# A hybrid attention and Mamba block on one core: first stage cut into halves and steps, small projection feature-major, decay mask moved to a multiplication

## What is computed

```
mod = silu(c) @ ada_w + ada_b            # six rows of 1024: shift, scale, gate, twice
h = rms_norm(x, g0) * (1 + sc_m) + sh_m
proj = h @ w_in                          # q, kv_lat (256), q_idx, k_idx (64), w_idx (8), z, xbc, dt_raw (32), gates
c_kv = rms_norm(kv_lat, kv_norm_g);  k_idx = rms_norm(k_idx, kidx_norm_g)
att = sparse attention over the 256 best keys of each query
# Mamba-2 in chunks of 128 tokens, per head:
a_cum = cumsum(dt * a)
decay = exp(where(l >= s, a_cum[l] - a_cum[s], -inf))
y_diag = (C B^T * decay) @ (x * dt)
x = x + gt_m * rms_norm(merged(att, ssd) @ w_out, g1);  x = x + gt_f * rms_norm(mlp(...), g3)
```

## Time and profile before

| what | before |
|---|---|
| median of 3 runs | 2412.16 us |
| the profiled execution, own time | 2412.21 us |
| its span | 2410.4 us |
| PE busy | 2327.9 us (97%) |
| DVE busy | 1328.8 us (55%) |
| ACT busy | 723.3 us (30%) |
| POOL busy | 953.3 us (40%) |
| chain that ended last, by engine | PE 90%, DVE 5%, issue 2%, ACT 2%, DMA 1% |
| granted TensorE clock, mean | 0.996 |

### The profile page before, as it was taken

The page is one execution under the profiler, slowest core; times in us unless marked ns, Lnnn a source line. Parts: engine busy times, 40 slices in busy tenths (PEclk is TensorE's granted clock), DMA queues, the critical chain, the costliest instruction groups (busy, mean ns, idle before and its releaser), DMA issues.

```text
span 2410.4 us, 31914 instructions
## 1 busy us (share of the span) xinstructions
PE 2327.9 (97%) x12022; PEld 1919.5 (80%) x12022; DVE 1328.8 (55%) x1956; ACT 723.3 (30%) x1362; POOL 953.3 (40%) x630
## 2 busy tenths in 40 slices
PE   3999999998999999999999999999999999999997
PEld 2977888885557988888887888899888888888886
DVE  4259999995657167585767555334532322322325
ACT  5144121105652234435365111035511212112112
POOL 2221233237672463654554344446332333233222
PEclk9999999999999999999999999999999999999999
DMA  7111452225652113131222553334211111111103
GB/s 274 36 35 45 148 183 87 93 91 168 202 172 68 40 62 127 45 138 46 88 101 102 182 175 119 109 106 162 84 35 53 52 52 35 52 52 40 47 35 79
DMA packets 144732, 230.30 MB, mean 96 GB/s; under 512 B 7956, under 2 KB 111732, under 8 KB 143604
## 3 DMA queue, kind: packets, MB, share of 16 engines
q1 hardware_dynamic: 119936, 166.11, 20.8%
q10 hardware_dynamic: 23684, 59.06, 6.4%
q0 software_dynamic: 1008, 3.67, 0.9%
HBM read 176.39 MB, written 52.43 MB: 95 GB/s over the span
## 4 chain that ended last, share of the span: by engine, by line
PE 90%; DVE 5%; issue 2%; ACT 2%; DMA 1%; ACTq 0%; DVEq 0%
PE ps L652 88%; DVE score L1737 2%; DVE probT L1820 1%; DVE mod_sum L1664 1%; PE ps L877 1%; PE ps L914 1%; PE ps L981 1%; ACT decay L1510 0%; PE ps L700 0%; DMA gate_d<-last_spill 0%; DMA rows_b<-in_ssm_norm_g_dram 0%; ACT L1510 0%; DVE prob L1803 0%; DVE acc L1959 0%; DVE a_lo L1873 0%
## 5 line engine op out<-in xcount | busy, mean ns | idle before, releaser
L652 PE MATMUL ps<-a_hi,w_hi 128*128 128x512 f32 x1728 | 676.7, 392 | 1.7 <-DVE a_lo L1873 1.2
L652 PE MATMUL ps<-a_lo,w_hi 128*128 128x512 f32 x1728 | 672.8, 389 | 0.0
L580 POOL CAST w_hi<-raw 128x2048 fp32r<-128x2048 f32 x90 | 174.7, 1941 | 1179.2 <-issue 859.2
L652 PE MATMUL ps<-a_hi,w_lo 128*128 128x512 f32 x1728 | 543.1, 389 | 0.0
L584 POOL TENSOR_TENSOR w_lo<-raw,w_hi 128x512 fp32r<-128x512 f32 (+1 forms) x360 | 521.5, 1481 | 7.2
L2029 DVE TENSOR_TENSOR x_tm<-x_tm,ps 128x1024 f32<-128x1024 f32 x120 | 146.5, 1221 | 453.8 <-PE ps L652 453.1
L652 PEld LDWEIGHTS ps<-a_hi,w_hi 128*128 128x128 f32 x1728 | 324.5, 188 | 69.6 <-DVE a_lo L1873 1.9
L652 PEld LDWEIGHTS ps<-a_hi,w_lo 128*128 128x128 f32 x1728 | 324.4, 188 | 67.9
L652 PEld LDWEIGHTS ps<-a_lo,w_hi 128*128 128x128 f32 x1728 | 324.5, 188 | 66.2 <-issue 0.2
L652 PE MATMUL ps<-w_hi,a_hi 128*128 128x256 f32 (+1 forms) x896 | 259.1, 289 | 4.4 <-DVE a_lo L1873 2.7
L652 PE MATMUL ps<-w_lo,a_hi 128*128 128x256 f32 (+1 forms) x896 | 253.6, 283 | 0.0
(11 more groups left out here) (255 smaller groups left out, 3033.1 us busy)
## 6 DMA issues: line engine op xcount, KB each, us to landing
raw<-in_w_in_dram SPq DMA_DIRECT2D x35, 1024.0 KB, 5.0
ada_raw<-in_ada_w_dram SPq DMA_DIRECT2D x16, 1024.0 KB, 8.7
raw<-in_w_up_dram SPq DMA_DIRECT2D x16, 1024.0 KB, 5.4
raw<-in_w_down_dram SPq DMA_DIRECT2D x16, 1024.0 KB, 4.7
gates<-gate_d SPq DMA_DIRECT2D x12, 1024.0 KB, 4.9
act_raw<-acts_d ACTq DMA_DIRECT2D x20, 512.0 KB, 5.4
ada<-in_ada_w_dram SPq DMA_DIRECT2D x8, 1024.0 KB, 20.5
acts_d<-decay ACTq DMA_DIRECT2D x16, 512.0 KB, 4.3
```

The source lines that it names most:

```text
L580: nc.gpsimd.tensor_copy(hi, src).then_inc(hi_made, 1)
L652: return nc.tensor.matmul(o, a, b, start=start, stop=stop)
```

## The change

1. SP loads tokens 0 to 511 first, then `ada_w` (its last piece in two halves), the kv block, and only then tokens 512 to 1023.
2. ACT squares, roots and scales the first four tiles; it squares the other four after that, and DVE scales these. `mod_sum`'s last product comes in two halves of 1024 columns, and PE sums each half as it comes. DVE reads the sums in PSUM itself; part of `gain` is made ahead.
3. PE turns six tiles before the sums (banks `FIRST_TURN`), then runs 60 more transposes whose result nobody reads (`IDLE_TURNS`), then the sums.
4. The kv projection goes by feature tiles (`kv_step`): tile `k` of the first four token tiles is multiplied as soon as its split is there, between the turns of the rest.
5. The small projection has its weights (104 columns) as the stationary operand and 512 tokens moving; ACT copies the result to `small_fm`, and PE turns it back (`small_turns`) inside the next block.
6. In `segments` the two `past_bf` matmuls are gone. ACT takes relu(a_cum[s] - a_cum[l]) from PSUM for 8 heads, then one exponential of minus that over 1024 columns. DVE multiplies bank 7 with the triangle `tri` into `cb_sb` in `mix_in`, which takes the place of ACT's copy.

```
-            for t in range(NT):
-                sp.dma_start(x_tm[:, t, :], x[0, t * P:(t + 1) * P, :]).then_inc(x_landed[t], 16)
+            load_tokens(range(4))
             for k in range(KT):
-                sp.dma_start(ada0[:, k, :], ...)
+                if k < KT - 1:
+                    sp.dma_start(ada0[:, k, :], ...)
+            for half in range(2):
+                c = slice(half * D, half * D + D)
+                sp.dma_start(ada0[:, KT - 1, c], ada_w[0, D - P:D, c]).then_inc(ada_last if half else ada_in[KT - 1], 16)
             load(0, cols(w, C_KV))
+            load_tokens(range(4, NT))
...
-            norm_turn(0, range(4))
-            pe.wait_ge(mod0_summed, 1)
+            norm_turn(0, range(6), banks=FIRST_TURN)
+            for i in range(IDLE_TURNS):
+                nc.tensor.transpose(ps[:, 1, (i % 4) * P:(i % 4 + 1) * P], x_tm[:, i % 4, 0:P], ident[:, :])
             for m in range(2 * KT):
-                last = mm(ps[:, 3, m:m + 1], mod_sum[:, m * P:(m + 1) * P], ones[:, 0:1], start=True, stop=True)
+                if m % KT == 0:
+                    pe.wait_ge(mod0_summed, m // KT + 1)
+                last = mm(ps[:, 0, m:m + 1], mod_sum[:, m * P:(m + 1) * P], ones[:, 0:1], start=True, stop=True)
...
+            def kv_step(k, tokens):
+                pe.wait_ge(h_split, tokens[0] // 4 * KT + k + 1)
+                for t in tokens:
+                    last = tm_token(0, t, ps[:, t // 2, (t % 2) * R:(t % 2) * R + R], R, ks=(k,), half=t % 2)
+                return last
+            for k in range(KT):
+                norm_turn(0, (6 + k,), banks=FIRST_TURN)
+                pe.wait_ge(w_split[0], k * LO_PARTS // KT + 1)
+                kv_step(k, range(4))
+            norm_turn(0, (14, 15), banks=FIRST_TURN)
+            for k in range(KT):
+                last = kv_step(k, range(4, NT))
...
-            for t in range(NT):
-                last = tm_token(1, t, ps[:, 4 + t // 4, (t % 4) * NSM:(t % 4) * NSM + NSM], NSM)
+            for k in range(KT):
+                wh, wl = (w_tile(w, 1, k, 0, NSM, NSM) for w in (w_hi, w_lo))
+                for q in range(2):
+                    r = slice(q * 512, q * 512 + 512)
+                    mm(ps[0:NSM, 6 + q, :], wh, a_hi[:, k, r], start=(k == 0))
+                    mm(ps[0:NSM, 6 + q, :], wh, a_lo[:, k, r])
+                for q in range(2):
+                    last = mm(ps[0:NSM, 6 + q, :], wl, a_hi[:, k, q * 512:q * 512 + 512], stop=(k == KT - 1))
...
                     if k >= 1:
-                        pe.wait_ge(decay_done, g * NT + k)
+                        pe.wait_ge(decay_done, 2 * (g * NT + k) - 1)
...
-                        mm(o.rearrange("p (h l) -> p h l", h=4), ident_bf[:, :],
-                           past_bf[:, :].rearrange("p (o l) -> p o l", o=1).broadcast_to([P, 4, P]), start=True)
...
-                        if k >= 1:
-                            act.wait_ge(mix_ready, g * NT + k)
-                        nc.scalar.copy(cb_sb[:, :], ps[:, 7, 0:P]).then_inc(cb_out, 1)
                         if k >= 2:
                             act.wait_ge(mix_done, g * NT + (k - 1))
                         for h in range(HG):
-                            ins = nc.scalar.activation(decay[k % 2][:, h, :], ps[...], ACT.Exp, bias=acum[...])
+                            ins = nc.scalar.activation(decay[k % 2][:, h, :], ps[...], ACT.Relu, bias=dta[...], scale=-1.0)
                         ins.then_inc(decay_done, 1)
+                        act.wait_ge(decay_done, 2 * (g * NT + k) + 1)
+                        nc.scalar.activation(decay[k % 2][:, :, :], decay[k % 2][:, :, :], ACT.Exp, scale=-1.0).then_inc(decay_done, 1)
...
-                    dve.wait_ge(decay_done, g * NT + (k + 1))
+                    dve.wait_ge(seg_done, g * NT + (k + 1))
+                    if g or k:
+                        dve.wait_ge(mix_ready, g * NT + k)
+                    ve.tensor_tensor(cb_sb[:, :], ps[:, 7, 0:P], tri[:, :], ALU.mult).then_inc(cb_out, 1)
+                    dve.wait_ge(cb_out, g * NT + (k + 1))
+                    dve.wait_ge(decay_done, 2 * (g * NT + k + 1))
                     ve.tensor_tensor(decay[k % 2][:, :, :], decay[k % 2][:, :, :],
                                      cb_sb[:, :]...broadcast_to([P, HG, P]), ALU.mult).then_inc(mix_ready, 1)
```

More of the change, by code:

```diff
@@ L677, in fm_block, with tm_token @@
                 return last
[L679 removed]
+            def tm_token(n, t, o, width, stationary=None, nk=KT, c0=0, wwidth=None, ks=None, half=None):
                 s = n % 2
@@ L686, in tm_token @@
                     wh, wl = (w_tile(w, s, k, c0, c0 + width, ww) for w in (w_hi, w_lo))
-                    mm(o, sh[:, k, r], wh, start=(k == 0))
+                    mm(o, sh[:, k, r], wh, start=(k == 0 and half != 1))
                     mm(o, sh[:, k, r], wl)
-                    last = mm(o, sl[:, k, r], wh, stop=(k == nk - 1))
+                    last = mm(o, sl[:, k, r], wh, stop=(k == nk - 1 and half != 0))
                 return last
@@ L735, in kv_turns, with small_turns @@
+            last.then_inc(w_used[1], 1)
+            def small_turns(k):
+                if k == 1:
+                    pe.wait_ge(kv_out, 1)
+                    for t in range(NT):
+                        last = nc.tensor.transpose(ps[:, 4 + t // 4, (t % 4) * NSM:(t % 4) * NSM + NSM],
+                                                   small_fm[:, t * P:(t + 1) * P], ident[0:NSM, 0:NSM])
+                    last.then_inc(rows_turned, 1)
             def kv_turns(k):
@@ L1670, in _ @@
             dve.wait_ge(roots, 1)
-            ve.reciprocal(stat[:, NT:2 * NT], stat[:, 0:NT]).then_inc(vars_ready, 1)
-            for k in range(1, KT):
+            ve.reciprocal(stat[:, NT:NT + 4], stat[:, 0:4]).then_inc(vars_ready, 1)
+            for k in range(1, KT - 1):
                 mod_product(k)
-            dve.sem_inc(mod0_summed, 1)
-            dve.wait_ge(c_ready, 2)
-            V.link(ve.tensor_tensor(mod[:, 0:16], mod[:, 0:16], vec_a[:, 0:16], ALU.add))
-            V.link(ve.tensor_scalar(gain[:, 0:KT], mod[:, 8:16], 1.0, None, ALU.add))
@@ L1678, in _ @@
-            ve.tensor_tensor(gain[:, 0:KT], gain[:, 0:KT], vec_a[:, 56:64], ALU.mult).then_inc(gain_ready, 1)
-            norm_split(0)
+            for half in range(2):
+                if half:
+                    dve.wait_ge(ada_last, 16)
+                else:
+                    dve.wait_ge(ada_in[KT - 1], 16)
+                c = slice(half * D, half * D + D)
+                ve.scalar_tensor_tensor(mod_sum[:, c], ada0[:, KT - 1, c], c_act[:, KT - 1:KT], mod_sum[:, c],
+                                        ALU.mult, ALU.add).then_inc(mod0_summed, 1)
@@ L1682, in _ @@
+            norm_split(0, range(2))
+            dve.wait_ge(roots, 2)
+            V.link(ve.reciprocal(stat[:, NT + 4:2 * NT], stat[:, 4:NT]))
+            for t in range(4, NT):
+                ve.tensor_scalar(x_tm[:, t, :], x_tm[:, t, :], stat[:, NT + t:NT + t + 1], None, ALU.mult).then_inc(normed, 1)
+                if t % 2:
+                    norm_split(0, (t // 2,))
+            norm_split(0, range(4, 2 * KT))
             dve.wait_ge(rows_in, 16 * 5)
```

94 lines of the change are left out of this document (49 added, 45 removed).

## The result

The changed kernel took **2377.57 us**, the median of 4 runs (2377.27 to 2378.86), against 2411.86 for the kernel before beside it (2411.45 to 2413.59). The ratio is 0.9855, 95% interval [0.9841, 0.9869]: 34.3 us less. Forecast were 2378.5 us, 2371 to 2389.

A forecast was written before the change was run, and what follows sets the result against it. TensorE (PE), busy for 97% of the span, was taken as the bound. From 2412.2 us: kv -9.6, small projection -10.5, turning back +0.9, SSD stage -14.5, giving 2378.5 us; range 2371 to 2389.

The forecast's parts named there:

- Kv projection, -9.6: First stage: the kv projection ends at 72.9 in place of 82.5 us, -9.6 us.
- two halves of 1.2 us at 34.1 and 35.3: DVE's products before the gain: the last comes in two halves of 1.2 us, ending at 34.1 and 35.3.
- If they run slow: PE's 16 sums before the gain: at the slow clock they end at 41.3 us, not 37.7.
- the 0.7 us for a slow start: Kv projection: PE may start slow after idling before the first split, between nothing and 1.5 us, taken as 0.7.
- Small projection, -10.5 and +0.9: Small projection: 48 matmuls take 10.9 in place of 21.4 us, -10.5; 8 transposes turning the result back add 0.9.
- both covers: Small projection: the kv_lat reading and the splitting of block 2's weights both fit below its 10.9 us, 2.4 to spare.
- 64 masks, -14.1, of which 0.8 is lost at chunk 5: SSD stage: dropping 64 mask matmuls of 0.22 us saves 14.1; DVE's y at chunk 5, groups 1 and 2, costs 0.8.
- Waits for decays, -4.1, and the group start, +2.9: SSD stage: PE's 4.1 us of waits go; later decays for the multiplication cost 2.9 over four group starts.
- with 1.7 us of multiplication 977.9: SSD group 1 start: decays at 976.2, multiplication done at 977.9, PE there at 977.4, so it loses 0.5 us.
- The idle turns stay slow: First-stage rival: turns of 0.23 us, kv ends at 81.7, -0.8 in place of -9.6; 2388 us, chance 0.12.
- Half of the masks' gain given back: SSD rival: half of the masks' gain is lost in chunks where DVE sets the pace; 2386 us, chance 0.09.
- Slower, by DVE: SSD loop rival: DVE becomes the bound, 1.5 us over in 32 chunks; 2441 us, chance 0.03.

The follow-up runs named there:

- masks_back: Changed kernel with the 64 mask matmuls back ahead of the segment matmuls, relu, exponential and masked copy left as changed; 2390.75 us, ratio 0.9911.
- ssd_back: Changed kernel with the whole SSD part as before (mask matmuls, exponential from PSUM, ScalarE's copy of C B^T); 2394.59 us, ratio 0.9930.
- no_idle: Changed kernel without the 60 idle turns (IDLE_TURNS = 0); 2378.70 us, ratio 0.9861.
- dve_op9: Changed kernel with nine more masked copies of C B^T on VectorE in each of the 32 SSD chunks; 2390.52 us, ratio 0.9908.
- pool_only: Changed kernel with GpSimd's split of the small block held back until x is scaled, no extra turns; 2376.59 us, ratio 0.9851.
- dve_op: Changed kernel with three more masked copies of C B^T on VectorE in each of the 32 SSD chunks; 2378.81 us, ratio 0.9863.
- turns_on: Changed kernel with 8 more idle turns between the halves of the sums and 24 behind them; 2378.96 us, ratio 0.9860.
- x_early: turns_on with the late x tiles loaded ahead of the kv block; 2381.93 us, ratio 0.9873.
- pool_later: turns_on with GpSimd's split of the small block held back until the second half of x is scaled; 2376.49 us, ratio 0.9851.
- h_first: turns_on with ACT's last two squares behind the first two h, and DVE's first split ahead of its wait for them; 2378.73 us, ratio 0.9862.
- first_back: Changed kernel with the first stage up to the kv projection as before, small projection and SSD part as changed; 2389.10 us, ratio 0.9903.

## Why the prediction was right, and where it wasn't

The time came 0.9 us below the forecast, and each part lies within 2 us of what it said. By its steps:

- **Kv projection, -9.6.** Measured -9.4. The sum was right by errors that cancelled. The step "two halves of 1.2 us at 34.1 and 35.3" failed in its second half: 36.9. The step "If they run slow" was not either-or: the first 16 sums were fast and the second 16 slow, ending at 40.5 instead of 37.7. The last x tile landed at 40.3, not 39.4, so that the first h came at 41.7, not 40.7; the gain was there at 41.0; x was scaled at 49.4, not 48.0. Against that, the 14 steps and 8 turns that were left took 23.7 us from the first of these turns (its row is `49.48 0.66 PE L709 MATMUL ps<-ident,x_tm 128*128 128x128 f32 x4 [0.79 <-DVE x_tm L1727]`) to 73.14, 0.5 less than the 24.2 worked out, and the 0.7 us for a slow start did not come on top, since the slow steps lay ahead of that wait. SP's queue held one thing that the sum did not have: it stood 17.29 us in the issue of an x tile (the chain's row `9.52 17.29 SPq L390`). No loss by it is seen, since the DMA engines stayed full: the window of that stretch reads `9.60:26.80 17.20, 4.46 (x24) 1.00 1.01 394`, a DMA share of 1.01.
- **Small projection, -10.5 and +0.9.** Measured 21.42 - 11.10 = -10.3, and 8 turns 0.7 us. 48 matmuls of 104 stationary columns kept the pace of block 2, and block 2 began with no wait: both covers held.
- **64 masks, -14.1, of which 0.8 is lost at chunk 5.** Measured by `masks_back` about -12.4 (three groups: 9.28). The part given back is somewhat larger than I had it (1.28 us in three groups, of which PE's two waits for y are 0.9). It was where the prediction put it in group 1: at 1009.90 PE waited 0.55 us for DVE's y of chunk 5.
- **Waits for decays, -4.1, and the group start, +2.9.** Measured together about -3.0 (`ssd_back` against `masks_back`), not -1.2. The wait went. The group start was mis-sized: "with 1.7 us of multiplication 977.9" took an operation at its slowed length. In group 1 relu, load, exponential (1.06, not 1.2) and multiplication (1.23) ended at 953.9, when PE came there, and PE's list has no wait for it.
- **Rivals.** *The idle turns stay slow* did not come true, and `no_idle` shows that 32 slow sums by themselves cost some 0.3 us or nothing at kv's end, where the bound had +2: in the forecast as in the trace the last square stands beside the sums, and x is scaled at 49.6 in `no_idle` against 49.4 although the gain comes 0.6 us later. What 60 slow turns ahead of them would cost was not run. *Half of the masks' gain given back:* 12% was. *Slower, by DVE:* 0.9 us more a chunk costs 0.4 us in three groups, so this rival, at 1.5 us over in all chunks, was far off.
- **Slips in the arithmetic that change nothing.** The first rival's own terms make 2387.3, not 2388, and so the sum by the Trainium skill's sentence would have been 8.8 us smaller, not 10. Both traces list 34 table loads of ACT, not 33; that they are equal is what the argument used.

The sentence of the Trainium skill that was cited ("TensorE: Matmul & The Clock Gate", Part 4, that the full clock does not engage in transposes) disagrees with this trace too: 60 turns of 0.11 us at a granted 1.00.

## What to carry to other kernels

A transfer that is moved forward brings its consumer forward too: ask what the engine behind it will then run beside. Time an engine's operations where it is alone, and look for the second engine wherever a row is longer. When the path to an end has two arms (here the sums, and the squares in ACT's queue), an edit that speeds up one is worth the difference between them and no more.

## What was unexpected of the hardware

**VectorE and GpSimd take turns, and who starts first wins.** In the changed kernel GpSimd's cast began at 33.93, 0.1 us before DVE's second half-product could, and took its usual 1.90 us; the two halves then took 4.11 us. In `no_idle` the half-product was first, the two took 2.48 and the cast 2.60. One stands still until the other is done: 33.93 + 1.90 + 1.24 = 37.07, near the 36.91 seen; and in `no_idle` 35.30 + 1.90 = 37.20, near the 37.05 at which its cast ends:

```profile
34.45 2.60 POOL L587 CAST w_hi<-raw 128x2048 fp32r<-128x2048 f32 x1 [31.78 <-DMA raw<-in_w_in_dram]
```

The Trainium skill, "SBUF — State Buffer", Who interferes with whom, calls the port pair that these two engines share an exclusive lock, and says that issue order decides who blocks. This trace agrees, by 2.9 us for a half-product in place of 1.24. Half a microsecond of arrival decides which of two engines pays. Of the eleven executions with these products in this place, DVE paid in four (4.11 to 4.17 us for its two halves), and GpSimd's cast in seven (2.52 to 2.94 us).

**The same 32 sums ran at either level.** In the changed kernel's execution, behind 60 turns at 1.00, the granted clock was 0.87 in the 3 us with the first 16 sums and a wait, and 0.50, the lower of the two levels (1.2 GHz of 2.4), with the second 16. The same sums behind the same 60 turns took 3.63 us for all 32 in `dve_op9`, at a granted 1.00, 4.60 in `pool_only` (1.00 until 36.4, 0.57 from there), and 5.25 and 5.29 in `dve_op` and `masks_back`. With 8 turns in the pause between, the second 16 took 1.8 to 2.1 us in three kernels (`turns_on`, `x_early`, `pool_later`) and 3.41 in `h_first`. So one execution doesn't tell the pace of such a stretch, and whether the 8 turns help is not shown. The granted clock alone doesn't tell it either: in the kernel before, the 32 sums took 6.99 us in a window that grants 1.00.

**An execution's end moves by itself.** From the first decays of group 3 to the end, the profiled executions whose SSD part is unchanged took from 1164.1 us (`pool_later`) to 1167.5 us (`first_back`). The cause stays open. An effect of 1 us can be read at a place inside the trace, not at its end.
